# First chunks' modulation and first strips in smaller transfers at the start of a two-block transformer kernel

## The reference

```python
c_act = jax.nn.silu(c)
mod = (jnp.einsum('bd,dn->bn', c_act, w_ada[l]) + b_ada[l]).reshape(b, N_SUB, 3, D_MODEL)
h = modulate(x, norm_w[l, 0], mod[:, 0, 0], mod[:, 0, 1])     # rms_norm(x, w) * (1 + scale) + shift
x = x + 0.5 * mod[:, 0, 2][:, None, :] * swiglu(h, ffn_w13[l, 0], ffn_w2[l, 0])
# swiglu(h, w13, w2): g, u = split(h @ w13); (silu(g) * u) @ w2
```

## Time and profile before

| | |
|---|---|
| median of 3 runs | 1744.08 us (1743.83 to 1744.18) |
| profiled execution, its own time | 1743.86 us |
| its span in the profile | 1742.1 us |
| TensorE busy | 1706.0 us, 98% |
| VectorE / ScalarE busy | 62% / 36% |
| moved from memory | 215.34 MB read, 125 GB/s over the span |
| in the first 56 us | some 310 to 350 GB/s in most stretches |

### The profile page before, as it was taken

One profiled execution on the slowest core, in us unless ns is written; L12 is line 12 of the kernel. 1 busy time (PEld: TensorE's weight loads), 2 busy tenths in 40 slices (PEclk: granted clock), 3 DMA queues, 4 the chain that ended last, 5 costly groups with the idle time before them and its releaser, 6 DMA issues.

```text
span 1742.1 us, 23533 instructions
## 1 busy us (share of the span) xinstructions
PE 1706.0 (98%) x8390; PEld 1397.5 (80%) x8390; DVE 1079.3 (62%) x1875; ACT 635.6 (36%) x934; POOL 66.7 (4%) x56
## 2 busy tenths in 40 slices
PE   7899999999999999999999999999999999999998
PEld 5688888887878867887888888888867888888887
DVE  4778678655746656559969973569685453434343
ACT  4321221234246553344222334442475342323241
POOL 0000000010000000200000000200001100000002
PEclk9999999999999999999999999999999999999999
DMA  9866666333423202537666632445201243333321
GB/s 319 252 206 198 185 195 199 108 100 94 117 62 96 84 1 64 164 111 211 189 208 192 173 102 79 139 138 129 65 1 37 62 120 95 99 94 99 95 86 49
DMA packets 357710, 218.42 MB, mean 125 GB/s; under 512 B 8544, under 2 KB 355716, under 8 KB 357636
## 3 DMA queue, kind: packets, MB, share of 16 engines
q1 hardware_dynamic: 357404, 217.37, 42.7%
q10 hardware_dynamic: 232, 0.09, 0.0%
HBM read 215.34 MB, written 2.11 MB: 125 GB/s over the span
## 4 chain that ended last, share of the span: by engine, by line
PE 92%; DVE 4%; SPq 1%; ACT 1%; issue 1%; DMA 1%; DVEq 0%; ACTq 0%
PE bank L699 26%; PE bank L700 26%; PE bank L701 26%; PE bank L740 1%; PE bank L741 1%; PE bank L744 1%; PE bank L870 1%; PE bank L859 1%; PE bank L929 1%; PE bank L787 1%; SPq L560 1%; PE bank L904 1%; DMA PBUF<-in_w_ada 1%; DVE W_LO L1554 1%; PE bank L1091 0%
## 5 line engine op out<-in xcount | busy, mean ns | idle before, releaser
L699 PE MATMUL bank<-H_HI,W_HI 128*128 128x512 f32 x1292 | 504.2, 390 | 6.5 <-DVE W_LO L1554 3.1
L701 PE MATMUL bank<-H_HI,W_LO 128*128 128x512 f32 x1292 | 502.7, 389 | 0.0
L700 PE MATMUL bank<-H_LO,W_HI 128*128 128x512 f32 x1292 | 502.7, 389 | 0.0
L1200 ACT ACTIVATE W_HI<-RAW 128x1024 fp32r<-128x1024 f32 x278 | 292.3, 1055 | 476.1 <-PE bank L701 453.3
L1554 DVE TENSOR_TENSOR W_LO<-RAW,W_HI 128x1024 fp32r<-128x1024 f32 x278 | 341.0, 1227 | 87.8 <-ACT W_HI L1200 78.4
L699 PEld LDWEIGHTS bank<-H_HI,W_HI 128*128 128x128 f32 x1292 | 242.5, 188 | 60.4 <-issue 4.0
L699 PE MATMUL bank<-A_HI,W_HI 128*128 128x512 f32 x736 | 287.1, 390 | 0.0
L701 PE MATMUL bank<-A_HI,W_LO 128*128 128x512 f32 x736 | 286.4, 389 | 0.0
L700 PE MATMUL bank<-A_LO,W_HI 128*128 128x512 f32 x736 | 286.3, 389 | 0.0
L701 PEld LDWEIGHTS bank<-H_HI,W_LO 128*128 128x128 f32 x1292 | 242.5, 188 | 50.5
L700 PEld LDWEIGHTS bank<-H_LO,W_HI 128*128 128x128 f32 x1292 | 242.5, 188 | 50.1 <-issue 0.2
(11 more groups left out here) (295 smaller groups left out, 1535.9 us busy)
## 6 DMA issues: line engine op xcount, KB each, us to landing
RAW<-in_ffn_w SPq DMA_DIRECT2D x116, 512.0 KB, 4.9
GBUF<-in_w_ada SPq DMA_DIRECT2D x32, 1024.0 KB, 7.4
RAW<-in_mlp_w SPq DMA_DIRECT2D x64, 512.0 KB, 3.8
RAW<-in_w_in SPq DMA_DIRECT2D x57, 512.0 KB, 3.9
GBUF<-in_ada_w SPq DMA_DIRECT2D x24, 1024.0 KB, 7.2
RAW<-in_w_out SPq DMA_DIRECT2D x16, 512.0 KB, 3.6
RAW<-in_ffn_w SPq DMA_DIRECT2D x16, 384.0 KB, 3.1
PBUF<-in_w_ada SPq DMA_DIRECT2D x4, 1024.0 KB, 10.0
```

Source lines behind the costliest of these rows:

```text
L699: pe.matmul(dst, w_hi, x_hi, start=first and i == 0, stop=False)
L700: pe.matmul(dst, w_hi, x_lo, start=False, stop=False)
L701: mm = pe.matmul(dst, w_lo, x_hi, start=False, stop=last and i == len(blocks) - 1)
L1200: act.activation(strip_of(W_HI, slot), strip_of(RAW, slot), ACT.Copy).then_inc(hi_ready, 1)
```

## The change

Five things are changed, all of them in the first 60 us or so.

1. The modulation weights of chunks 0 to 3 are loaded one chunk at a time (`load_chunk`: two transfers of 512 KiB with rows of 128 columns). Chunks 4 to 7 stay in pairs.
2. The first strips arrive in three parts of 2, 2 and 4 chunks (`load_part`) and are split in these parts: part 0 where the first half was, part 1 (all slots) behind chunk 1, part 2 behind chunks 2 and 3 (two slots each). The queue is now: x, rows, chunk 0, part 0, chunk 1, chunk 2, part 1, chunk 3, pair 2, part 2, pair 3.
3. TensorE takes `modulate(0)` as soon as the first bank of x is copied, ahead of the turned columns and `spread`; the copies of x are divided and ordered anew, Sqrt stands ahead of ScalarE's copies.
4. In chunk 7 the products of strips 0 and 1 with H_HI are put ahead of the wait for H_LO.
5. In the first turn Silu of strip 0 stands ahead of the split of strip 4 on ScalarE, and HF ahead of W_LO of strip 4 on VectorE.

The number of products and the bytes moved are the same, but for 8 fewer tiny warming matmuls.

```diff
-        X_ACT = (0, 4, 6)
+        X_DVE, X_ACT = (0, 3, 2, 1, 5), (4, 6, 7)
...
+        def first_in(k):
+
+            if k < 4:
+                return [(pe_gem_in[k], 32)]
+            return [(gem_in[k // 2 * 2 - 4 + i], 16) for i in range(2)]
+
+        FIRST_PARTS = ((0, 2), (2, 4), (4, KC))
...
+            def load_chunk(k):
+
+                tile = first_pair(k // 2).rearrange("p (s k n) -> p s k n", s=2, k=KC)
+                for i in range(2):
+                    at = i * D + k * P
+                    sp.dma_start(tile[:, i, :, k % 2 * P:(k % 2 + 1) * P], w_ada[:, :, at:at + P]).then_inc(pe_gem_in[k], 16)
...
+            def load_part(part):
+
+                lo, hi = FIRST_PARTS[part]
                 for j in range(RING):
+                    col = j // 2 * P + j % 2 * FF
+                    sp.dma_start(first_part(RAW, j, part).rearrange("p (k n) -> p k n", k=hi - lo),
+                                 w13[0][:, lo:hi, col:col + P]).then_inc((first_raw[0], first_raw[1], raw_in)[part][j], 16)
...
-            load_pair(0)
-            load_halves(0)
-            load_pair(1)
-            load_halves(1)
+            load_chunk(0)
+            load_part(0)
+            load_chunk(1)
+            load_chunk(2)
+            load_part(1)
+            load_chunk(3)
             load_pair(2)
+            load_part(2)
             sp.wait_ge(x_turned, KC)
             sp.wait_ge(xsq_done, TT)
             load_pair(3)
...
                 for k in range(KC - 1):
                     modulate(k + 1)
-                    if k == 0:
-                        pe.wait_ge(first_hi, RING)
+                    if k in (0, 2):
+                        pe.wait_ge(first_hi, RING + k // 2 * RING)
...
+                k = KC - 1
+                at = [slice(s * STRIP + k * P, s * STRIP + (k + 1) * P) for s in range(RING)]
                 pe.wait_ge(each[0], each[1] + KC)
+                for s in range(2):
+                    pe.matmul(bank[s][:, :], W_HI[:, at[s]], chunk(hi, k), start=False, stop=False)
+                    pe.matmul(bank[s][:, :], W_LO[:, at[s]], chunk(hi, k), start=False, stop=False)
                 pe.wait_ge(each[2], each[3] + KC)
-                for s in range(RING):
-                    products(bank[s][:, :], s, [(KC - 1, KC - 1)], hi, lo, S, first=False).then_inc(strip_done, 1)
+                for s in range(2):
+                    pe.matmul(bank[s][:, :], W_HI[:, at[s]], chunk(lo, k), start=False, stop=True).then_inc(strip_done, 1)
+                for s in range(2, RING):
+                    products(bank[s][:, :], s, [(k, k)], hi, lo, S, first=False).then_inc(strip_done, 1)
...
+            pe.wait_ge(x_dve, 1)
+            modulate(0)
             pe.wait_ge(const_ready, 4)
             pe.wait_ge(rows_in, 16 * 14)
-            pe.wait_ge(x_dve, 3)
+            pe.wait_ge(x_dve, 2)
...
+            pe.wait_ge(x_dve, 3)
             spread(warm=0)
-            pe.wait_ge(x_act, 1)
-            keep_warm(8)
-            modulate(0)
+            pe.wait_ge(x_dve, 4)
             keep_warm(4)
...
                     for p in range(2):
+                        first = split and p == 0
                         for j in (2 * p, 2 * p + 1):
-                            if j >= split:
+                            if not first:
                                 split_next(u0, it, j)
                         g = u0 + 2 * p
                         act.wait_ge(strip_done, it * RING + (g + 1 + RING))
                         act.activation(SG[:, p * S:(p + 1) * S], bank[g % RING][:, :], ACT.Silu).then_inc(silu_ready, 1)
+                        if first:
+                            split_next(u0, it, split)
...
+            act.activation(RMS[:, 0:TT], STAT[:, 208:208 + TT], ACT.Sqrt, bias=CONST[:, 0:1], scale=1.0 / D).then_inc(std_ready, 1)
             copy_x(X_ACT[0])
-            act.activation(RMS[:, 0:TT], STAT[:, 208:208 + TT], ACT.Sqrt, bias=CONST[:, 0:1], scale=1.0 / D).then_inc(std_ready, 1)
+            first_rows(0)
...
             def between_chunks(k):
 
                 if k + 1 < KC:
                     first_rows(k + 1)
-                if k in (1, 2):
-                    first_halves(1, (0, 1) if k == 1 else (2, 3))
+                if k == 1:
+                    first_parts(1)
+                if k in (2, 3):
+                    first_parts(2, (0, 1) if k == 2 else (2, 3))
...
-                        split_next(u0, it, 2 * c + (skip and c == 0), 2 * per)
+                        if c or not skip:
+                            split_next(u0, it, 2 * c, 2 * per)
...
-                        if c or not skip:
-                            split_next(u0, it, 2 * c + 1, 2 * per)
+                        split_next(u0, it, 2 * c + 1, 2 * per)
```

More of the change, by code:

```diff
@@ L265, in block_pair_kernel @@
         xsq_done = sem("xsq_done")
-        first_raw = [sem(f"first_raw{i}") for i in range(RING)]
+        first_raw = [[sem(f"first_raw{q}_{i}") for i in range(RING)] for q in range(2)]
         first_hi = sem("first_hi")
@@ L420, in block_pair_kernel, with first_part @@
         X_ORDER = (6, 7, 4, 5, 0, 1, 2, 3)
-        X_ACT = (0, 4, 6)
+        X_DVE, X_ACT = (0, 3, 2, 1, 5), (4, 6, 7)
         def first_pair(p):
             return (GBUF[:, 0:2 * KC * GEM], GBUF[:, 2 * KC * GEM:4 * KC * GEM], PBUF[:, 0:2 * KC * GEM], PBUF3[:, :])[p]
-        first_in = gem_in + pe_gem_in
-        def first_half(t, slot, half):
-            return t[:, slot * STRIP + half * STRIP // 2:slot * STRIP + (half + 1) * STRIP // 2]
+        def first_in(k):
[3 more added lines that the diff above has]
+        FIRST_PARTS = ((0, 2), (2, 4), (4, KC))
+        def first_part(t, slot, part):
+            lo, hi = FIRST_PARTS[part]
+            return t[:, slot * STRIP + lo * P:slot * STRIP + hi * P]
         def shift_and_scale(t, k):
@@ L553, in load_pair @@
                 for i in range(2):
-                    sp.dma_start(tile[:, i, :, :], ada(p + i * TT)).then_inc(first_in[2 * p + i], 16)
-            def load_halves(half):
+                    sp.dma_start(tile[:, i, :, :], ada(p + i * TT)).then_inc(gem_in[2 * p - 4 + i], 16)
+            def load_part(part):
+                lo, hi = FIRST_PARTS[part]
                 for j in range(RING):
-                    src = w13[0][:, half * KC // 2:(half + 1) * KC // 2, j // 2 * P + j % 2 * FF:j // 2 * P + j % 2 * FF + P]
-                    sp.dma_start(first_half(RAW, j, half).rearrange("p (k n) -> p k n", k=KC // 2),
-                                 src).then_inc((first_raw, raw_in)[half][j], 16)
+                    col = j // 2 * P + j % 2 * FF
+                    sp.dma_start(first_part(RAW, j, part).rearrange("p (k n) -> p k n", k=hi - lo),
+                                 w13[0][:, lo:hi, col:col + P]).then_inc((first_raw[0], first_raw[1], raw_in)[part][j], 16)
             for i in range(TT):
@@ L760, in begin @@
                     turn_modulation(k + 1)
-                    if k == 0:
-                        pe.wait_ge(first_lo, RING)
+                    if k in (0, 2):
+                        pe.wait_ge(first_lo, RING + k // 2 * RING)
                     for s, cut in enumerate(at):
@@ L1138, in modulate @@
                 p, c = k // 2, k % 2
-                pe.wait_ge(first_in[2 * p], 16)
-                pe.wait_ge(first_in[2 * p + 1], 16)
+                for landed, count in first_in(k):
+                    pe.wait_ge(landed, count)
                 tile = first_pair(p).rearrange("p (s k n) -> p s k n", s=2, k=KC)
@@ L1473, in first_rows, with first_parts @@
                 act.activation(GROW[:, k % 2 * GEM:(k % 2 + 1) * GEM], bank[6 + k % 2][:, 0:GEM], ACT.Copy).then_inc(grow_ready, 1)
-            def first_halves(half, slots=range(RING)):
+            def first_parts(part, slots=range(RING)):
                 for j in slots:
-                    act.wait_ge((first_raw, raw_in)[half][j], 16)
-                    act.activation(first_half(W_HI, j, half), first_half(RAW, j, half),
-                                   ACT.Copy).then_inc((first_hi, hi_ready)[half], 1)
+                    act.wait_ge((first_raw[0], first_raw[1], raw_in)[part][j], 16)
+                    act.activation(first_part(W_HI, j, part), first_part(RAW, j, part),
+                                   ACT.Copy).then_inc((first_hi, first_hi, hi_ready)[part], 1)
             for t in range(TT):
@@ L1490, in _ @@
             act.sem_inc(bank_free, RING)
-            first_rows(0)
-            first_halves(0)
+            first_parts(0)
             def between_chunks(k):
@@ L2069, in copy_x @@
                 dve.tensor_copy(chunk(X, X_ORDER[n]), bank[X_ORDER[n]][:, :]).then_inc(x_dve, 1)
-            for n in (1, 2, 3):
+            for n in X_DVE[0:2]:
                 copy_x(n)
             token_factors()
-            for n in (5, 7):
+            for n in X_DVE[2:]:
                 copy_x(n)
@@ L2082, in _, with first_parts @@
             dve.wait_ge(x_dve, KC - len(X_ACT))
```

(8 more changed lines are left out.)

## The result

The changed kernel takes 1747.74 us (median of 20 runs, 1745.04 to 1749.23); the kernel before took 1744.00 in its 20. The ratio is 1.0018, with a 95% interval of 1.0012 to 1.0024: slower by 3.7 us, or 0.2%. That lies in the range of the forecast (1741.6 to 1748.0), 0.3 us inside its end, and 3 us above its value, next to rival 2's 1747.3.

The account below looks back on a forecast made before the run. TensorE, busy 98% of the span, was taken as the bound, so only its idle time counts. A +3.2 us wait ahead of chunk 3 and -2.5 us in the tail gave +0.7 on 1744.0: 1744.7, range 1741.6 to 1748.0.

Parts of the forecast that it names:

- rival 2: TensorE does little from about 34 to 40.4 us, so the clock falls: +3.3 us in all, 1747.3; chance 0.15.
- What stands in the queue: Ahead of chunk 3: 9.5 MiB needed, 0.5 less than before, but 4 MiB of w_ada in 512 B rows.
- when chunk 3 can start: Last part's slot 1 lands at 37.1, chunk 3's products follow 3.3 later at 40.4, not 37.23: +3.2 us.
- Price of the smaller rows: Start's queue: 4 MiB of w_ada in 512 B rows take 2.7 us extra, between nothing and 4.8.
- The tail: Chunk 7 to strip 5: with the table load hidden, strip 5 starts at 64.7 against 67.15, -2.5 us.
- The sum: Whole kernel: +3.2 - 2.5 = +0.7 us, counted from 1744.0, gives 1744.7.
- Bytes alone: Start's queue: the smaller rows cost nothing, chunk 3 starts at 37.7, total 1742.0; chance 0.15.
- Crawling transfers: Chunks and parts between x and pair 2 (5 MiB) move under 247 GB/s; at 230 GB/s 1749.1; chance 0.10.
- The last part not waited for: TensorE sets the pace from 20.4 on, chunk 3 starts at 33.7, total 1738.0; chance 0.07.
- The tail not shortened: End of the first phase: the table load waits for the product, total 1745.9; chance 0.03.

Follow-up runs that it names:

- the kernel with the late splits: The changed kernel with the last part's splits of all four slots behind chunk 3, none behind chunk 2: 1741.50 us, ratio 0.9987.
- the tail alone: The kernel before with items 4 and 5 of the change and nothing else: 1741.11 us, ratio 0.9982.
- the front alone: The changed kernel with items 4 and 5 of the change taken back: 1749.44 us, ratio 1.0026.
- the mixed kernel: The changed kernel with chunks 2 and 3 in a pair, the last part's four splits behind chunk 3, 8 warming products ahead of modulation 0: 1742.49 us, ratio 0.9989.
- the mixed kernel with more warming: The mixed kernel with 8 more warming products in the wait ahead of the modulation of chunk 2: 1741.50 us, ratio 0.9984 to the kernel before.

## Why the prediction came out as it did

**What stands in the queue, and when chunk 3 can start: right, the exact figure by luck.** The last part's slot 1 was put at 37.1 and came at 37.2. The chain behind it was put at 3.3 and took 3.2. Chunk 3 was put at 40.4 and came at 40.42. In four later profiles of the same queue the slot came between 36.0 and 36.8 and chunk 3 started at 39.2 to 40.0, always some 3.2 us behind it. So the mechanism held each time, and the term was +2.0 to +2.8 there in place of +3.2. Chunk 0's start, put near 20.4, came at 23.55 in the first profile, behind a wait of 3.0 us for its weights and at the lower clock, and at 20.32 in the second, and as the prediction said it made no difference. That the place of the split causes this, and not the transfers for chunks 4 and 5, the kernel with the late splits shows: chunk 3 at 35.65.

**Price of the smaller rows: right in kind, its size within what the profiles allow.** The term was 2.7 us; 2.0 separates the landings with small and with large rows in two kernels that ran beside each other (286 against 332 GB/s in the same window), and the five profiles with small rows give 2.0 to 3.2. The estimate from the Trainium skill, "DMA: Bandwidth & Descriptors", section "Why small descriptors are slow (HBM only)", was 1.0, so the smaller transfers cost more in this kernel than the page's cost per packet gives. That the cost is one per packet isn't shown.

**The tail: right.** It was put at -2.5, and the timelines show -2.4 in the changed kernel and -2.45 alone. The assumption that the table load runs during the wait held. The medians give -3.1 alone and -2.4 as what the changed kernel loses without it. In the profile of the tail alone an earlier landing made up the difference (0.8 us); whether it does in the median isn't shown.

**The sum: this step failed, by leaving out the clock.** The forecast was +0.7, and the clock stood beside it as rival 2 at a chance of 0.15. The gap ahead of chunk 3 came just as the steps said, and in all three profiles with that gap unfilled (the changed kernel twice, its front once) the clock fell in or behind it, at a price of 1.6, 3.0 and 1.7 us for chunk 3's step. With 14 small products in the gap the step is 4.42 and 4.44 and the time +0.4 and 0.0 against the kernel before. That this is close to the +0.7 of the sum is in part chance: in these two profiles chunk 3 started 2.3 and 2.0 us later than before and not 3.2, and the attention's lower clock added 1.3 to each. The rival's price of 2.6 lies among the three that were found; its chance was too low. A gap longer than any in the trace of before, with only the small products of one modulation in front, should have been the likeliest case and not the unlikely one. The time lies in the range because the range took this rival in, and not because the sum was right. The section of the Trainium skill that I cited for it, "HAM oscillation — how this bites in real kernels" in "TensorE: Matmul & The Clock Gate", says that a long wait for a transfer sets the array back to half speed, and these three profiles agree with it.

**The other rivals.** Bytes alone: falls, by 286 against 332 GB/s. Crawling transfers: fall, the window of 21.3 to 26.6 us of the changed kernel moved 296 GB/s, and that of 8 to 20 us 261, where the rival needed less than 247. The last part not waited for: falls in the changed kernel, but the kernel with the late splits is its picture, at 1741.5 and not the 1738.0 that I gave, since pair 2 lands at 34.6 and the splits still cost 1.3. The tail not shortened: falls.

**What isn't shown.** The lower clock at the end of the attention made 2.7 us in the first profile. It is found in four of the five profiles of kernels that hold the wait ahead of chunk 3 (the changed kernel once of twice, both with warming at chunk 3, the front alone) and in none of the other seven, the kernel before among them. That hints at a connection with the change, which no run tests, and a part of the 3.7 us may be this. The one try to warm the attention was in a kernel whose profile without the warming didn't show the fall. Items 1 to 3 of the change were not taken apart but for the size of the rows and the place of the splits.

## What to carry to other kernels

A split or a copy that waits for a later transfer, put in the stream of an engine that also makes the next operand, delays that operand by the whole wait; put it behind the last operand that doesn't need it. Smaller transfers bring the first data sooner and all the rest later, so look at what the queue must have delivered by the first point at which the compute engine sets the pace. Count a gap on TensorE twice, once for its length and once for the matmuls behind it (here 3.6 us and then 1.6, or 3.8 and then 3.0), and try to fill it with small products if it can't be closed: ahead of chunk 3 that kept the clock, in the mixed kernel the fall only came at another wait.

## What the runs showed that I had not expected

The fall of the clock needs less of a gap than the one that was forecast. It came behind a wait of 2.29 us that followed a full chunk of products at full speed (chunk 1's step 5.98 for 4.42) and in one of 2.35 us in the mixed kernel with more warming. With the attention warmed it came in chunk 0's products near 23.5, where the waits of the ten microseconds before are 0.79 and 1.18 us long. Waits of 2.35 us in the earlier trace rows and of 1.6 us before strip 4 left it alone, and so did the same wait of 1.18 us ahead of chunk 0 in the earlier trace rows. So the length of a single wait doesn't tell in these traces whether the clock falls. The same program can meet it in one execution and not in the next. The runs of one kernel spread by 1.5 to 4.2 us; how much of that is the clock isn't shown. Landings of the same queue vary by about 1 us between executions (slot 1 at 36.0, 36.1, 36.3, 36.8 and 37.2). And with the tail alone there is a version faster than both kernels: 1741.1 us, 0.18% below the one before.
